# Gates of the sparse experts: scattered into a zeroed grid in DRAM and multiplied in from there, in place of one-hot matmuls

## What is computed

```
s1, i1 = top_k(s[..., 0, :], 16)          # of 128 keys, per token and head (8 heads)
s2, i2 = top_k(s[..., 1, :], 16)
cand, cidx = s1 + s2, i1 * 128 + i2       # 256 candidates per head
top_s, pos = top_k(cand, 16)
idx = cidx at pos;  g = softmax(top_s)    # 128 experts and gates per token
act = gelu(h . u[idx])
out = sum over the 128 of (g * act) * v[idx]
```

## Time and profile before

| | us |
|---|---|
| median of 3 runs (2079.01 to 2079.53) | 2079.11 |
| the profiled execution | 2080.71 |
| its span, first to last instruction | 2078.9 |
| PE busy | 2045.3 |
| DVE busy | 1707.5 |
| ACT busy | 1169.6 |
| POOL busy | 315.9 |

### The profile page before, as it was taken

How to read it: one execution, slowest core, us unless ns; L and a number is a source line. 1 busy time by engine, 2 the same in 40 slices (tenths; PEclk the granted TensorE clock), 3 DMA queues, 4 the chain that set the end, 5 groups by cost and what they waited for, 6 DMA issues and landing times.

```text
span 2078.9 us, 37457 instructions
## 1 busy us (share of the span) xinstructions
PE 2045.3 (98%) x11366; PEld 1726.2 (83%) x11366; DVE 1707.5 (82%) x3094; ACT 1169.6 (56%) x2324; POOL 315.9 (15%) x265
## 2 busy tenths in 40 slices
PE   6999999999999999999999999999999999999997
PEld 3578888668999988888888888888888888888886
DVE  4467777897778788888877888888789999989997
ACT  3332225576455555555565666666666666666666
POOL 0000000000000000000010211111355554323320
PEclk9999999999999999999999999999999999999999
DMA  9978887400778555556577744445799999999992
GB/s 386 408 264 305 278 287 277 155 1 28 273 257 310 186 185 188 185 189 187 187 274 261 222 162 161 161 161 187 249 359 374 367 360 360 344 354 369 390 347 99
DMA packets 161063, 524.87 MB, mean 252 GB/s; under 512 B 34992, under 2 KB 35808, under 8 KB 160352
## 3 DMA queue, kind: packets, MB, share of 16 engines
q1 hardware_dynamic: 123984, 452.63, 60.6%
q0 software_dynamic: 20576, 67.20, 9.3%
q10 hardware_dynamic: 16432, 4.19, 0.9%
HBM read 515.52 MB, written 8.39 MB: 252 GB/s over the span
## 4 chain that ended last, share of the span: by engine, by line
PE 94%; DVE 3%; ACT 1%; DMA 1%; issue 1%; DVEq 0%; SPq 0%; ACTq 0%
PE PS L944 23%; PE PS L1332 23%; PE PS L1337 12%; PE PS L1384 6%; PE PS L1386 6%; PE PS L1385 6%; PE PS L1389 6%; PE PS L1388 6%; PE PS L1320 2%; PE PS L1014 1%; DVE st L1644 1%; PE PS L1147 1%; PE PS L931 1%; DMA ada_t<-w_ada 1%; PE PS L1119 1%
## 5 line engine op out<-in xcount | busy, mean ns | idle before, releaser
L508 ACT ACTIVATE w_hi<-raw 128x512 fp32r<-128x512 f32 x1088 | 681.1, 630 | 654.2 <-PE PS L944 258.5
L1436 DVE TENSOR_TENSOR w_lo<-raw,w_hi 128x512 fp32r<-128x512 f32 x1088 | 730.7, 690 | 228.7 <-ACT w_hi L508 203.7
L1332 PE MATMUL PS<-h,w_hi 128*128 128x512 f32 x2048 | 562.9, 396 | 0.0
L1332 PEld LDWEIGHTS PS<-h,w_hi 128*128 128x128 f32 x2048 | 349.7, 189 | 46.6
L1337 PEld LDWEIGHTS PS<-h,w_lo 128*128 128x128 f32 x2048 | 313.7, 189 | 43.7
L1337 PE MATMUL PS<-h,w_lo 128*128 128x256 f32 x2048 | 325.4, 281 | 0.0
L1384 PE MATMUL PS<-w_hi,p_hl 128*128 128x512 f32 x512 | 199.5, 390 | 0.6 <-DVE p_hl L2021 0.4
L1386 PE MATMUL PS<-w_hi,p_hl 128*128 128x512 f32 x512 | 199.2, 389 | 0.0
L1385 PE MATMUL PS<-w_hi,p_hl 128*128 128x512 f32 x512 | 199.2, 389 | 0.0
L1389 PE MATMUL PS<-w_lo,p_hl 128*128 128x512 f32 x512 | 199.2, 389 | 0.0
L1388 PE MATMUL PS<-w_lo,p_hl 128*128 128x512 f32 x512 | 199.2, 389 | 0.0
(11 more groups left out here) (266 smaller groups left out, 3143.0 us busy)
## 6 DMA issues: line engine op xcount, KB each, us to landing
raw<-stream SPq DMA_DIRECT2D x544, 512.0 KB
ada<-w_ada SPq DMA_DIRECT2D x112, 512.0 KB, 5.0
raw_far<-stream SPq DMA_DIRECT2D x104, 512.0 KB
ada_t<-w_ada SPq DMA_DIRECT2D x64, 512.0 KB, 8.2
ada_u<-w_ada SPq DMA_DIRECT2D x16, 512.0 KB, 4.5
values_scratch<-A ACTq DMA_DIRECT2D x1, 2560.0 KB
x_c<-x_ctx SPq DMA_DIRECT2D x1, 2048.0 KB, 7.9
x<-x_lat SPq DMA_DIRECT2D x1, 2048.0 KB, 15.4
```

Of the source, the lines that this page charges most:

```text
L508: nc.scalar.activation(w_hi[:, (2 * j + hf) % SPLIT, :], ring[:, j, hf * HALF:(hf + 1) * HALF], ACT.Copy).then_inc(S["w_high"], 1)
L1332: mm(PS[:, i, :], w_hi[:, h % SPLIT, q * P:(q + 1) * P], h2[:, :, k, :], start=(k == 0), stop=False, skip_group_check=True)
L1436: V_.tensor_tensor(w_lo[:, h % SPLIT, :], ring[:, h // 2 % RAW, at_:at_ + HALF], w_hi[:, h % SPLIT, :].bitcast(F32), ALU.subtract).then_in ...
```

## The change

The routing goes. A tensor `grid` in DRAM (128 x 128 x 192 floats, 12.58 MB) has a cell for each expert and dense token. Eight DMAs of SP fill it with zeros, in the queue behind the first four units of the output projection. The top 16 of the tokens t = 0 are normalised and turned to addresses early (in the second part's search), and POOL issues 128 indirect DMAs that add one gate per token each into the grid; then 64 more for tokens 128 to 191, each of 128 cells too, after moving half of the slots to partitions 64 to 127 with two small DMAs. After each head's DMAs POOL waits until they have landed, since two heads may choose the same expert. Then POOL loads the grid back, two tiles at a time (64 DMAs of 128 x 2 x 192 floats, two buffers `gt`), and DVE multiplies each pair of tiles by it (`gate_tiles`), four pairs per turn in turns 48 to 63 and after. Gelu now goes straight into A for all tiles.

```diff
+            sp.wait_ge(S["const_ready"], 4)
+            cells = grid.rearrange("p i t -> p (i t)").rearrange("p (r z) -> p r z", z=P)
+            n_cells = NE_TILES * DENSE // P // ZERO_PARTS
+            for r in range(ZERO_PARTS):
+                sp.dma_start(cells[:, r * n_cells:(r + 1) * n_cells, :],
+                             zeros[:].bitcast(F32).unsqueeze(1).broadcast_to([P, n_cells, P])
+                             ).then_inc(S["grid_zeroed"], 16)
...
+            def scatter_gate(address, value, done):
+                nc.gpsimd.indirect_dma_start(cells, bass.IndirectOffsetOnAxis(ap=address, axis=0), value, None,
+                                             compute_op=ALU.add).then_inc(done, 16)
+            pool.wait_ge(S["grid_zeroed"], 16 * ZERO_PARTS)
+            pool.wait_ge(S["gates_ready"], 1)
+            for h in range(HEADS):
+                if h:
+                    pool.wait_ge(S["scattered0"], 16 * TOPK * h)
+                for k in range(h * TOPK, (h + 1) * TOPK):
+                    scatter_gate(addr0[:, k:k + 1], sel[:, 0, 2, k:k + 1], S["scattered0"])
+            pool.wait_ge(S["gates_ready"], 2)
+            half_slots = lambda a: a.rearrange("p (h k) -> p h k", k=TOPK)[0:PICKED, :, TOPK // 2:TOPK]
+            nc.gpsimd.dma_start(addr1[PICKED:P], half_slots(sel[:, 1, 0, :].bitcast(U32))).then_inc(S["halves_moved"], 16)
+            nc.gpsimd.dma_start(gate1[PICKED:P], half_slots(sel[:, 1, 2, :])).then_inc(S["halves_moved"], 16)
+            pool.wait_ge(S["halves_moved"], 32)
+            pool.wait_ge(S["scattered0"], 16 * TOPK * HEADS)
+            for h in range(HEADS):
+                if h:
+                    pool.wait_ge(S["scattered1"], 16 * TOPK // 2 * h)
+                for k in range(TOPK // 2):
+                    scatter_gate(addr1[:, h, k:k + 1], gate1[:, h, k:k + 1], S["scattered1"])
+            pool.wait_ge(S["scattered1"], 16 * TOPK // 2 * HEADS)
             pool.wait_ge(S["picks_ready"], 1)
             for a, dst in enumerate((row_near, value_at, gate_at)):
                 nc.gpsimd.dma_start(dst[0:PICKED], near[PICKED:P, a, :]).then_inc(S["picks_in"], 16)
...
+            for c in range(NE_TILES // 2):
+                if c >= 2:
+                    pool.wait_ge(S["gated"], c - 1)
+                nc.gpsimd.dma_start(gt[:, c % 2], grid[:, 2 * c:2 * c + 2, :]).then_inc(grid_in[c % 2], 16)
...
-                        if routing and h % 4 == 1:
-                            route(2 * b + (i - 2 * b0), i)
...
+            def gate_tiles(c, q):
+                dve.wait_ge(grid_in[q % 2], 8 * c + (16 - 8 * (q % 2)))
+                dve.wait_ge(S["gelu_done"], 2 * c + 4)
+                pair = A[:, bass.ds(2 * c, 2), 0:DENSE]
+                V_.tensor_tensor(pair, pair, gt[:, q % 2], ALU.mult).then_inc(S["gated"], 1)
...
+            def gating_turn(b):
+                for s in range(2):
+                    c = 4 * b + (2 * s - 4 * GATED_AT)
+                    tile_lows(b + (34 + s), 3 - 2 * s, 2 * b + s, s, lambda: gate_tiles(c, 0))
+                    gate_tiles(c + 1, 1)
...
+EXP_AT, GATES_AT = 15, 30
+GATED_AT = 48
+ZERO_PARTS = 8
-VALUES_AT = 120
+VALUES_AT = (80, 120)
```

More of the change, by code:

```diff
@@ L214, in block_program @@
         row_t = at("row_t", [P, ROWS, D], F32, R + 128 * KB)
[L215 to L221, removed]
+        row_far = i1T[:, 0:PICKED].bitcast(U32)
+        picked, weight, fold = i2T[:, 0:PICKED], gT[:, 0:PICKED], gT[:, PICKED:2 * PICKED]
         ada_u = at("ada_u", [P, ADA, UNIT], F32, R + 112 * KB)
@@ L1311, in _, with first_product @@
             pe.wait_ge(S["sc_kept"], 2)
-            def route(g, s):
-                pe.wait_ge(S["hot_a"], g + 1)
-                pe.wait_ge(S["hot_b"], g + 1)
-                pe.wait_ge(S["routed"], g + 1)
-                for q in range(4):
-                    ins = mm(PS[:, 4 + s, q * P:(q + 1) * P], hotB[:, q, :], hotA[:, q, :], start=True, stop=True)
-                ins.then_inc(S["route_used"], 1)
-            def first_product(b0, n, routing=False):
+            def first_product(b0, n):
                 with pe.Fori(b0, b0 + n) as b:
@@ L1902, in _ @@
                         ada_keep_turned(6, 6)
+                    if t == 1 and k == 1:
+                        normalise(0)
+                    if t == 1 and k == 2:
+                        addresses(0)
+                        dve.sem_inc(S["gates_ready"], 1)
                 link(V_.tensor_copy(if16[:], ix16[:]))
@@ L1925, in _ @@
                     next_low(5)
[L1927 to L1931 removed]
+                over_top(t)
             up = slice(PICKED, P)
@@ L1942, in _ @@
             next_low(2)
-            link(V_.tensor_tensor(spare[up], ident[up], iota[up], ALU.mult))
-            link(V_.reduce_sum(place[up], spare[up], AX))
-            link(V_.tensor_scalar(place[up], place[up], -float(PICKED), None, ALU.add))
             link(V_.scalar_tensor_tensor(spare[up], first, 2.0 * P, second, ALU.mult, ALU.add))
@@ L1949, in _ @@
             next_low(3)
-            link(V_.scalar_tensor_tensor(spare[up], second, float(NE_TILES), first, ALU.mult, ALU.add))
+            experts(1)
             both_parts(1, value_at, lambda dst, c: V_.tensor_scalar(
-                dst.bitcast(U32), spare[up, c:c + PICKED], float(PICKED), place[up, 0:1], ALU.mult, ALU.add))
+                dst.bitcast(U32), spare[up, c:c + PICKED], float(PICKED), place[up, 2:3], ALU.mult, ALU.add))
+            addresses(1)
             next_low(2 * (U_U + 2 + 4 * GATES_AT + 2) - half[0])
-            dve.wait_ge(S["top_exp"], 1)
-            for t in range(QT):
-                link(V_.reduce_sum(gs[:, t, 1, :], ge[:, t], AX))
-                link(V_.reciprocal(gs[:, t, 1, :], gs[:, t, 1, :]))
-                link(V_.tensor_tensor(sel[:, t, 2, :].rearrange("p (h k) -> p h k", h=HEADS), ge[:, t],
-                                      gs[:, t, 1, :].unsqueeze(2).broadcast_to([P, HEADS, TOPK]), ALU.mult))
-                next_low(2 - t)
+            normalise(1)
+            low_slots = lambda a: a.rearrange("p (h k) -> p h k", k=TOPK)[0:PICKED, :, 0:TOPK // 2]
+            V_.tensor_copy(addr1[0:PICKED], low_slots(sel[:, 1, 0, :].bitcast(U32)))
+            link(V_.tensor_copy(gate1[0:PICKED], low_slots(sel[:, 1, 2, :])))
             dve.sem_inc(S["gates_ready"], 1)
+            next_low(3)
             both_parts(2, gate_at, lambda dst, c: V_.tensor_copy(dst, gate[:, c:c + PICKED]))
@@ L2082, in _ @@
             p_low(1, 1)
+            gate_tiles(63, 1)
             dve.wait_ge(S["picks_in"], 48)
```

198 lines of the change are left out of this document (69 added, 129 removed).

## The result

The kernel became slower: 2103.82 us median of 4 runs (2102.99 to 2106.47) against 2079.32 (2079.01 to 2080.15) for the kernel before beside it, a ratio of 1.0117 with an interval of 1.0105 to 1.0129. Forecast was 2036. The profiled execution took 2106.47 us, its span is 2104.6.

What follows compares the result with a forecast made beforehand. TensorE, busy 98% of the span, was taken as the bound; 43.7 us of routing work removed plus 0.5 us DVE lag gave -43.2 us, so 2036 us (own range 2033 to 2041; over the cases 2032 to 2082).

Steps and rivals of the forecast that it cites:

- 192 x 1.5 = 288 us: POOL's queue: issuing 192 adding indirect DMAs at 1.5 us each, taken from copy rows plus a little for the add.
- late from 1.65, no gain left from 1.88: POOL's scatter: above 1.65 us per add the grid is late; at 1.88 the whole 43 us gain is gone.
- the adding DMA costs double: Rival on POOL's scatter: doubled issue work, 2.2 us apiece gives 2141 us, 2.56 gives 2210; chance 0.20.
- 16 waits for landing: POOL waiting for DMAs to land between heads and at the parts' ends: 2.4 us each, 38 us.
- reserve of 29 us: POOL's queue: grid ready at 1225, 29 us ahead of DVE's first gate multiply.
- due time: DVE reaching the first gate multiply in turn 48, when the grid must be loaded: about 1254 us.
- The rule of the Trainium skill: Adding in DMA engines needs a second read descriptor, halving the rate; priced as doubled issue, the change sums to +62 us.
- sum of -43 us: Whole kernel: -43.7 us of removed TensorE routing work plus 0.5 us of DVE lag, -43.2 us.
- The zeros: SP's queue: eight DMAs, 12.58 MB, 44 us at 286 GB/s, hidden under attention; cost nothing.
- The grid loads: Loading the grid back: 3.2 to 5.6 us with multiply and wake against 5.61; rival that loads set the pace, 0.07.
- The search: DVE in the search: about twelve small added operations, some 3 us; lag from nothing to 1.5, taken as 0.5 us.
- ACT's part: Second exponential in the search: two more table changes on ACT, 1.28 us each; cost nothing.

Runs made afterwards that it cites:

- e2: Changed kernel without its 192 scatters and their waits; zeroing, grid loads and gate multiplies stay: 2040.72 us, ratio 0.9805.
- e12: e10 repeated unchanged on another chip, beside the plain scatter: 2039.73 us, ratio 0.9811.
- e7: Changed kernel with only the heads of the two parts issued in turn; gating still from turn 48, two buffers: 2074.36 us, ratio 0.9979.
- e4: Changed kernel with the second part's 64 adding DMAs moving 64 cells each in place of 128: 2092.6 us in one execution.
- e8: Changed kernel with gates multiplied in from turn 53, three pairs a tile, four buffers, and only the second part's first head written, not added: 2043.11 us, ratio 0.9823.
- e13: e6 repeated unchanged on another chip: 2041.07 us, ratio 0.9815.
- e6: Changed kernel with gates multiplied in from turn 53, three pairs a tile, four buffers, and both parts' first heads written, not added: 2049.75 us, ratio 0.9850.
- e9: e5 with the first head of both parts written, not added: 2051.67 us, ratio 0.9860.
- e10: Changed kernel with all 192 DMAs copying, not adding, and the second part's 64 moving 64 cells each in place of 128: 2226.39 us in one execution.
- e1: Changed kernel with the 192 indirect DMAs writing their gate in place of adding it: 2039.48 us, ratio 0.9801.
- e11: e1, the plain scatter, repeated unchanged on another chip: 2039.45 us, ratio 0.9807.
- e5: Changed kernel with gating from turn 53, three pairs a turn, four buffers, and the two parts' heads alternating from head 5: 2039.32 us, ratio 0.9804.

## Why the prediction was wrong

**The failed step** is the term "192 x 1.5 = 288 us" in the work of POOL's queue, and in it the sentence that the 4 B row is nearest, "plus a little for the add". An adding DMA takes 1.55 us to issue in the median where a copy takes 0.96, and with its idle time 1.96 us in the mean: (214.3 + 101.0 + 61.0)/192. The forecast had named the points itself: late from 1.65, no gain left from 1.88. The case that came is the side of its rival "the adding DMA costs double", slower from 1.88 on, though the issue did not double: 2.2 us apiece would have been 2141 by its sum, and 1.96 gives 2095. The other 9 us to 2104 are mainly the waits for landing, 48.5 us for 38. The rival had 0.20. The sign that the forecast gave for it, an add "over 1.58 us busy", is met by the mean (1.64) and not by the median (1.55).

From the forecast's 1225 to the 1323.9 measured, term by term:

| term | forecast | measured | difference |
|---|---|---|---|
| start of the scatter | 890 | 892.9 | +3 |
| 192 DMAs | 288 | 376.3 | +88 |
| 16 waits for landing | 38 | 48.5 | +11 |
| moves and `near` | 4.5 | 3.3 | -1 |
| first grid load | 4 | 3.0 | -1 |

The waits are 24.7, 17.2, 4.9 and 1.7: 2.2 to 4.9 us each while the stream ran, 1.7 to 1.9 once it stood still. The price of an issue alone (+88) used up the reserve of 29 us and 59 more; the waits gave the rest of DVE's 67.5 us, the due time being 2.5 later than forecast. TensorE, with the halves that were still buffered, stood 63.5 of them.

**The rule of the Trainium skill.** "Collectives: The Full Stack", section "The bandwidth ceiling: the fold count and why AG ≠ RS ≠ AR", had an add slow by its second read, in a collective that moves large chunks. Its direction is what came. Its size, taken as the price of an issue, is not: 1.55 against 0.96 is a factor of 1.6, and the 0.51 us that stay with half the cells do not go with a second descriptor for every cell. No run here shows how long the read and add themselves take in DRAM, or what the longer issue is made of; with the add or without it POOL waited 42 us for landing between heads.

**What was right.** The removed work and the sum of -43 us: with the scatter gone or cheap the span is 2036.0 or 2037.0, where 2035.7 was forecast, and the medians are 2 to 3 us above that sum. The zeros were covered by attention. SP's queue, where the forecast had the next load at 511 as before:

```profile
386.80 37.98 SPq L355 DMA_DIRECT2D grid_scratch<-zeros  x8
...
509.89 4.71 SPq L347 DMA_DIRECT2D raw<-stream  x2
```

A gate multiply took 0.55 us, as forecast. The grid loads held the pace. For line 482, POOL's own waits, who waited for it, and the landing:

```profile
L482 POOL DMA_DIRECT2D gt<-grid_scratch x64: 546/546/606, 1321.0 to 1494.5; - x64
...
  DVE A L1983: 73.4, 9
DMA to landing us min/median/max: 2.6/3.7/6.3
```

Of the 73.4 us, 67.5 are the first wait; the other eight come to 6, and TensorE shows no gap behind them. The due time was right to 2.5 us, and in e2 the second product begins at 1431.6, where the forecast had 1431.

**Small terms that were off.** The search was given 0.5 us and cost 3.8. DVE stood 3.65 us for ScalarE's exponential, which had a function table to load first, and TensorE had a gap of 2.19 us at 889, with two halves slow after it, at a granted clock of 0.53 (889.1 to 891.5):

```profile
884.12 1.28 ACT L819 ACT_TABLE_LOAD   x1
885.42 0.31 ACT L819 ACTIVATE ge<-tops 128x128 f32<-128x128 f32 x1
```

```profile
885.76 0.29 DVE L1867 TENSOR_REDUCE gs<-ge 128x8 f32<-128x128 f32 x1 [3.65 <-ACT ge L819]
```

```profile
889.10 1.12 PE L1310 MATMUL PS<-h,w_lo 128*128 128x256 f32 x4 [2.19 <-DVE w_lo L1397]
```

The forecast had judged ACT's part by its share of busy time and put it at nothing; what cost was where the exponential stood in ACT's order and who waited for it. The same gap is in e2, whose span came out right, so as much was gained elsewhere: its first product begins 1.9 us earlier than before (707.8 for 709.7), and the rest I did not trace. The second product takes 607.1 us (1497.5 to 2104.6) against 604.7 before; in e2 it takes 604.5, so the 2.4 us belong to the stalled kernel. The sum: 2036.0 of e2 + 63.5 + 2.1 + 2.4 = 2104.0, and the span is 2104.6.

## What to carry to other kernels

When a change puts a long chain of small DMAs on one queue against a due time, the price of one issue times their number is the forecast; where the trace has no row for that very kind, an error of 30% in it (1.96 for 1.5 us, 88 us in all) can be twice the whole gain, and the chance should say so. Such a chain that is late costs its lateness once, so before giving it up look for the cheap remedies: ask for the result later with more work per turn, and issue something independent while a dependent group lands; here these two turned a loss of 24 us into a gain of 39 to 41. Ask of every element whether it needs the dearer form: the first write to a zeroed cell needs no add.

## What the runs showed of the hardware

- Issue of an indirect DMA of 4 B cells by GpSimd, shortest: 0.953 us for 128 cells and 0.886 for 64 when it copies, 1.535 and 1.397 when it adds in DRAM, and 0.30 us idle between two in most cases. Half the cells save 7% of a copy and 9% of an add; of the add's surcharge 0.51 of 0.58 us stays. Beside the stream, 64 copied cells had a median of 1.03 (e12), no less than 128.
- TensorE, busy without a break before, ran its next halves at the lower level (1.2 GHz, granted clock 0.50 to 0.54; groups of up to 1.22 and 1.91 us for 0.63 and 1.09) after gaps of 2.2, 10.9, 30.5 (e7), 49.8 (e4) and 63.5 us. The loss behind them was 1.6, 1.7, 2.7, 1.8 and 2.1 us: it did not grow with the gap. After gaps of 0.85 (e8) and 1.85 us (e13) the granted clock stayed 1.00 and at most 0.2 us was lost.
- In three executions that were profiled (e6, e9, e10) ScalarE paused, 4 us three times in the first and up to 21.8 us in the last, while GpSimd issued plain indirect writes 1.26 us apart; TensorE and VectorE stood with it, and the DMA engines had nearly nothing to do (0.02 busy from 910 to 915 us in e6). The same three kernels on other chips had no pause (2041, 2040 and 2040 us in place of 2050, 2052 and 2226), nor did e1 and e11 with 192 such writes, nor any kernel that only adds, 1.85 us apart. All four executions of e6 (2047 to 2052) and of e9 (2051 to 2053) were slow, and all four of each repetition fast, so it is hardly the chance of a single execution; but e5 and e7, which only add, had no pause on e6's chip. On the two chips with pauses each stretch of plain writes had them, in the profiled executions: of 1.6 to 3.0 us with eight writes (e6, e8, e9), of 3.7 to 5.1 with sixteen (e6, e9), and growing from 2 to 21.8 us in the course of 128 (e10). What they come from is open: that they need the plain writes fits all these runs but is not shown, and neither is what in the chip or the session decides.
